# Half of the output matrix loaded during the RWKV recurrence, the other half first in the output stage

## What is computed

```python
mla_o = _mla_attend(q_nope, q_rope, kv[..., :MLA_NOPE], k_rope, kv[..., MLA_NOPE:])
hg_o, hg_s = _hgrn_mixer(hg_cols, p['hg_lb'], p['hg_norm'], hg_s0)
rw_o, rw_s = _rwkv_mixer(rw_cols, p['rw_mu'], p['rw_w0'], ..., rw_s0)
mix = jnp.concatenate([mla_o, hg_o, rw_o], axis=-1) @ p['w_out']
x = _layernorm(DEEPNORM_ALPHA * x + g1 * mix, p['ln_g'][0], p['ln_b'][0])
h2 = x * (1 + sc2) + sh2
ffn = _expert_choice(h2, p['router'], p['ex_w1'], p['ex_w3'], p['ex_w2'])
x = _layernorm(DEEPNORM_ALPHA * x + g2 * ffn, p['ln_g'][1], p['ln_b'][1])
```

## Time and profile before

| | before |
|---|---|
| timed runs, median (range) | 3454.83 us (3450.43 to 3464.23) |
| profiled execution, its own time | 3457.51 us |
| span of the profiled execution | 3455.7 us |
| mean granted TensorE clock | 0.91 |
| busy: TensorE, VectorE, GpSimd, ScalarE | 2651.1, 1272.5, 682.6, 475.0 us |
| output matmuls (line 1979) in both layers: busy, idle before them | 142.9 us, 25.1 us |
| what ended that idle time | the load of `w_out` |

### The profile page before, as it was taken

One profiled execution on the slowest core, in us unless ns is written; L12 is line 12 of the kernel. 1 busy time (PEld: TensorE's weight loads), 2 busy tenths in 40 slices (PEclk: granted clock), 3 DMA queues, 4 the chain that ended last, 5 costly groups with the idle time before them and its releaser, 6 DMA issues. The chain is left out here.

```text
span 3455.7 us, 87591 instructions
## 1 busy us (share of the span) xinstructions
PE 2651.1 (77%) x40000; PEld 2021.6 (58%) x40000; DVE 1272.5 (37%) x2847; ACT 475.0 (14%) x973; POOL 682.6 (20%) x844
## 2 busy tenths in 40 slices
PE   5998883748584888888979988566585858888886
PEld 1555553638534777777725545355484457777774
DVE  1101568784523112211240026786744231112114
ACT  0102332032101000000010023302211100000001
POOL 0000908334221000000010027272430200000001
PEclk9999997869886999999999999877798879999998
DMA  8300000000053988888671010000003458888872
GB/s 350 125 25 36 1 1 11 1 7 4 3 219 139 363 339 338 308 333 325 248 301 61 4 36 1 9 3 7 2 3 123 182 188 321 344 343 335 337 287 105
DMA packets 69616, 532.75 MB, mean 154 GB/s; under 512 B 13920, under 2 KB 15776, under 8 KB 32896
## 3 DMA queue, kind: packets, MB, share of 16 engines
q1 hardware_dynamic: 66176, 516.66, 38.4%
q0 software_dynamic: 3072, 10.49, 1.1%
HBM read 518.34 MB, written 8.79 MB: 153 GB/s over the span
## 5 line engine op out<-in xcount | busy, mean ns | idle before, releaser
L2285 PE MATMUL ps<-arena 128*64 128x80 f32 x16384 | 620.0, 235 | 107.3 <-issue 102.6
L2285 PEld LDWEIGHTS ps<-arena 128*64 128x64 f32 x16384 | 596.0, 139 | 130.0 <-issue 128.4
L2300 PE MATMUL ps<-arena 128*64 128x80 f32 x8192 | 324.2, 234 | 55.5 <-issue 53.8
L2300 PEld LDWEIGHTS ps<-arena 128*64 128x64 f32 x8192 | 304.0, 138 | 66.0 <-issue 65.7
L526 PE MATMUL ps<-arena 128*128 128x128 f32 (+1 forms) x1088 | 296.4, 435 | 5.3 <-DVE arena L579 5.3
L2470 DVE TENSOR_TENSOR arena<-arena,ps 128x160 f32<-128x160 f32 x128 | 41.2, 322 | 653.4 <-ACT arena L2390 653.4
L526 PEld LDWEIGHTS ps<-arena 128*128 128x128 f32 x1088 | 164.8, 192 | 137.0 <-issue 131.2
L2044 POOL DMA_INDIRECT arena<-h_d,arena x32 | 39.8, 1243 | 1025.9 <-DVEq L2411 920.9
L2390 ACT ACTIVATE arena<-ps 128x160 f32<-128x160 f32 x128 | 38.8, 303 | 1132.8 <-PE ps L2285 1132.8
L583 DVE COPY arena<-ps 128x128 f32<-128x128 f32 (+3 forms) x48 | 16.3, 341 | 399.4 <-PE ps L526 287.6
L1979 PE MATMUL ps<-arena 128*128 128x512 f32 x320 | 142.9, 610 | 25.1 <-DMA arena<-in_w_out 25.1
(11 more groups left out here) (345 smaller groups left out, 4065.3 us busy)
## 6 DMA issues: line engine op xcount, KB each, us to landing
arena<-in_ex_w SPq DMA_DIRECT2D x128, 2048.0 KB, 9.1
arena<-in_ex_w SPq DMA_DIRECT2D x128, 1024.0 KB, 9.2
arena<-in_ada_w SPq DMA_DIRECT2D x24, 2048.0 KB, 15.5
arena<-in_w_t SPq DMA_DIRECT2D x34, 512.0 KB, 3.5
arena<-in_w_out SPq DMA_DIRECT2D x4, 2048.0 KB, 10.3
arena<-in_w_tok SPq DMA_DIRECT2D x2, 3712.0 KB, 16.9
h_d<-x_sb SPq DMA_DIRECT2D x10, 512.0 KB, 2.6
arena<-in_w_uq SPq DMA_DIRECT2D x2, 1536.0 KB, 6.5
```

What stands on the lines that cost most here:

```text
L2285: m = nc.tensor.matmul(gated(j)[c * 64:(c + 1) * 64, f, a, :], w13[q % WG][:, a, k, f * P + c * 64:f * P + (c + 1) * 64], xT[:, x % 2, k, ...
L2300: m = nc.tensor.matmul(product(j)[c * 64:(c + 1) * 64, b, :], w2[:, q % WP, f, b * P + c * 64:b * P + (c + 1) * 64], he[:, x % 2, f, :], s ...
```

## The change

`w_out` is laid out in memory with each column half contiguous (16 KB in each partition). The first half is loaded in the RWKV stage, once SyncE has seen the last update of the inverse (`xy` = 25): its slices 0 to 5 go to the words of `rwT` from `a1` + 4 x 643, and slices 6 and 7 to the 1024 words of `hgT` from `a0` + 2560. The semaphore `ld_wo0` lives over both layers and is never cleared, so TensorE waits for 32 more in each layer. In the output stage the second half is the first request of SyncE, then the gate and norm rows, and only then come the clears, ahead of the expert weights. The small tiles of the stage lie elsewhere in the arena; their instructions are the same.

```diff
-        "w_out": f("w_out"), "ln_g": f("ln_g"), "ln_b": f("ln_b"),
+        "w_out": f("w_out").reshape(DEPTH, KD, P, 2, 512).transpose(0, 2, 3, 1, 4), "ln_g": f("ln_g"), "ln_b": f("ln_b"),
@@ phase_rwkv, SyncE
             sp.dma_start(S0, d["s_rw"][l].rearrange("d a p v -> p (d a) v")).then_inc(S["ld_rw"], 16)
+            sp.wait_ge(S["xy"], LVC * TILES)
+            k = 0
+            for dst in first_half(e):
+                n = dst.shape[1]
+                sp.dma_start(dst, d["w_out"][l, :, 0, k:k + n, :]).then_inc(S["ld_wo0"], 16)
+                k += n
             sp.wait_ge(S["rw_fin"], 1)
@@
+def first_half(e):
+
+    return e.part(e.a1 + 4 * PAD, 6, 512)[0], e.part(e.a0 + 4 * P * TILES, 2, 512)[0]
@@ phase_output
-    z = e.a0
-    wo, z = e.part(z, 2, KD, 512)
-    brow, z = e.part(z, 2, DM)
-    gb, z = e.part(z, 2, DM)
-    y, z = e.part(z, 2, DM)
+    wo_a, wo_b = first_half(e)
+    brow, z = e.part(e.a0, 2, DM)
     st, z = e.part(z, TILES, 16)
+    assert z <= e.a0 + 4 * P * TILES
+    gb, z = e.part(e.a0 + 4 * P * TILES + 2 * 512, 2, DM)
+    assert z <= e.a1 + 4 * PAD
+    y, z = e.part(e.a1 + NRW * PAD, 2, DM)
+    wo_1, z = e.part(z, KD, 512)
@@ SyncE
-            e.clear_last(sp)
-            for n in range(2):
-                sp.dma_start(wo[:, n], d["w_out"][l].rearrange("(k p) n -> p k n", p=P)[:, :, n * 512:(n + 1) * 512]
-                             ).then_inc(S[f"ld_wo{n}"], 16)
+            sp.dma_start(wo_1, d["w_out"][l, :, 1]).then_inc(S["ld_wo1"], 16)
             load_gate_rows(e, sp, 0, brow, S["n1ld"])
             load_norm_rows(e, sp, 0, gb, S["n1ld"])
+            e.clear_last(sp)
@@ TensorE
-                    if t == 0:
-                        pe.wait_ge(S[f"ld_wo{n}"], 16)
+                    if t == 0 and n == 0:
+                        pe.wait_ge(S["ld_wo0"], 32 * (l + 1))
+                    if t == 0 and n == 1:
+                        pe.wait_ge(S["ld_wo1"], 16)
```

More of the change, by code:

```diff
@@ L266, in program @@
         S = {n: sem(n) for n in ("ld_cond", "st_y")}
-        S.update({n: ctx.enter_context(nc.semaphore(n)) for n in ("ld_const", "ld_x0", "ld_x1") + EXPERT_WEIGHT_SEMS + MODULATION_WEIGHT_SEMS})
+        S.update({n: ctx.enter_context(nc.semaphore(n)) for n in ("ld_const", "ld_x0", "ld_x1", "ld_wo0") + EXPERT_WEIGHT_SEMS + MODULATION_WEIGHT_SEMS})
         e = Shared()
@@ L1931 @@
 OUTPUT_SEMS = (
-    "n1x", "op_ps", "op_ev", "st_x", "n1ld", "n1var", "n1sd", "n1nm", "n1xn", "ld_wo0", "ld_wo1",
+    "n1x", "op_ps", "op_ev", "st_x", "n1ld", "n1var", "n1sd", "n1nm", "n1xn", "ld_wo1",
 )
@@ L1975, in _ @@
                 for n in range(2):
-                    if t == 0:
-                        pe.wait_ge(S[f"ld_wo{n}"], 16)
+                    if t == 0 and n == 0:
+                        pe.wait_ge(S["ld_wo0"], 32 * (l + 1))
+                    if t == 0 and n == 1:
+                        pe.wait_ge(S["ld_wo1"], 16)
                     for k in range(KD):
-                        m = nc.tensor.matmul(ps[:, 2 * (t % 4) + n, :], e.mixT[:, k, t * P:(t + 1) * P], wo[:, n, k, :],
+                        half = wo_1[:, k, :] if n else wo_a[:, k, :] if k < 6 else wo_b[:, k - 6, :]
+                        m = nc.tensor.matmul(ps[:, 2 * (t % 4) + n, :], e.mixT[:, k, t * P:(t + 1) * P], half,
                                              start=k == 0, stop=k == KD - 1)
```

## The result

| | before | after |
|---|---|---|
| timed runs, median (range), 7 each | 3454.83 us (3450.43 to 3464.23) | 3428.47 us (3422.20 to 3440.66) |
| ratio, 95% interval | | 0.9923 (0.9909 to 0.9938) |
| span of the profiled execution | 3455.7 us | 3429.4 us |
| output matmuls in both layers: busy, idle before them | 142.9, 25.1 us | 142.8, 2.1 us |

The change saves 0.77%, 26 us; the forecast was 3432.2 us, 0.65% less. In two later comparisons the same kernel came out at 0.9939 (0.9925 to 0.9952) and 0.9935 (0.9916 to 0.9953) of the kernel before. The mean of the three ratios, 0.9932, is 23.4 us of 3454.8, and the forecast was 22.6.

A forecast was written before the change was run, and what follows sets the result against it. TensorE's stall before each layer's first output matmul, ended by the matrix load, was taken as on the path. 3457.5 - 11.5 - 11.1 = 3434.9, less 2.7 for the median, gave 3432.2 us; range 3425 to 3443.

The forecast's parts named there:

- The seam: Between RWKV and output stages, TensorE starts at the barrier instead of the load: gains 11.54 and 11.07 us, 22.6 together.
- The path argument: Output stage is TensorE-bound, so an earlier start moves tiles, barrier and rest of layer equally; the stall counts fully, twice.
- The term of the barrier: Gap from RWKV's last instruction to TensorE's first output matmul, taken as 0.5 us from the preceding seam's 0.28 and 0.69.
- The second half: Requested first in the output stage, lands after 8.2 us, before the first matmul group's 10.2 and 9.3 us end.
- Rival 1: Second half takes 12.8 us to land, stalling TensorE 3.0 and 3.9 us inside tile 0; 3439.1 us; chance 0.13.
- The estimate of 6.8 us: Second half's landing time by the skill's 2.0 us plus bytes / 436 GB/s; the sum would stay unchanged.
- The other requests: Output stage's gate and norm rows, last out near 954.0, and expert weights, near 958.6, behind the clears; cost 0.
- The recurrence: In the RWKV stage, the early load slows nothing: 0, with a far bound of 2 us a layer.
- The clock: At the output stage's start, low clock keeps costing 3.36 and 2.44 us; twice as long a stretch costs 5.8 us.
- a bound of 3.2 us: No low-clock stretch in tile 0 would gain 5.8 us, less the second half late by 1.3 us twice.
- Rivals 2 and 3: 2: TensorE tied elsewhere or experts' stage returns gain, near 3451, chance 0.07; 3: clock stays low, 3563, chance 0.03.

The follow-up runs named there:

- The run with the clears ahead: Changed kernel with the 64 semaphore clears put back ahead of the output stage's requests; 3436.82 us, ratio 0.9947.
- eight times the data: Changed kernel with each of the two pieces of the first half loaded eight times in the recurrence, 16 MB instead of 2 MB; 3429.84 us, ratio 0.9927.
- the 15 dummies: Changed kernel plus 15 unused matmuls on TensorE between the RWKV stage's transposes of the final state and of the result; 3429.32 us, ratio 0.9934.
- The run with 96 transposes: Changed kernel with both halves loaded early and 96 dummy transposes of a constant in place of the 15 dummy matmuls; single run 3426.39 us.
- with both halves early: Changed kernel with 15 dummy matmuls and the second half requested at the recurrence's end; 3423.66 us, ratio 0.9917; again 3426.97 us, 0.9920.
- seven dummies: Changed kernel with both halves loaded early and 7 dummy matmuls instead of 15; single run 3425.32 us.
- the order alone changed: Kernel before with the 64 clears moved after the matrix and row requests, nothing loaded early; 3453.76 us, ratio 0.9990.

## Why the prediction was right

**The seam.** 22.6 us forecast, 22.98 measured. The path argument held: all of it reached the end of the stage, whose rest kept its length (86.01 and 85.46 us). The term of the barrier was sized at 0.5 us between 0.28 and 0.69, and was 0.32 and 0.31; this 0.4 us is the only error in the sum proper.

**The second half.** Forecast to be in time by 2.0 and 1.1 us, with 7.8 us to landing and 0.4 for the issue. It landed 7.2 and 7.4 us after its request, and no wait is seen. The run with the clears ahead measured what happens without the margin: 2.13 and 1.07 us of wait. Rival 1 is refuted: its 12.8 us belonged to a load that had 2 MB ahead of it. The estimate of 6.8 us used a fit that the Trainium skill, "DMA: Bandwidth & Descriptors", section "Anatomy of one DMA — SWDGE (gpsimd) path", gives for loads issued by GpSimd. These are issued by SyncE, and the measured 7.2 to 7.4 us decide; by either figure the load is hidden.

**The other requests.** They cost nothing, as forecast, but were sized too long. The last norm row went out at 949.01 and not near 954.0, and landed 12.0 us later, at 961.0, 3 us before tile 0 was done. The expert weights were asked for from 953.42 on, against 958.6 forecast.

**The recurrence.** Forecast at 0 with 2 us a layer as the far bound; eight times the data showed 0.01 and 0.06 us between two profiles with the same clock. The forecast did not name what goes with a longer recurrence, a low clock at its start: 83.76 us beside 79.38 in two profiles of the changed kernel.

**The clock.** Forecast unchanged. Tile 0 changed by -0.30 and +0.08 us. The size was right: the 15 dummies show that the level at the seam is set by TensorE's rest of 12.7 us before the transposes, which the change leaves as it was, and not by the pause of the seam. That the low stretch could be removed, which I had only as a bound of 3.2 us, turned out to be worth 6.6 to 6.9 us, because the transposes of the result speed up too (1.1 us a layer) and the second half can be moved as well. The dummies alone gave 5.3. My sentence that the 0.50 in the transposes agrees with the Trainium skill, "TensorE: Matmul & The Clock Gate", part "PE-mode transpose", was a weak reading: they stood low because TensorE had rested ahead of them, and ten of them are over in 2.4 us. The run with 96 transposes speaks against the rule for 32-bit transposes in this kernel, as far as keeping the clock at 1.00 goes; that transposes alone raise it from 0.50 no run here shows.

**Rivals 2 and 3.** The seam is ended by the barrier, the experts' stage is not longer (table below), and the clock rose after 5.5 us: both are out.

**What the sum does not hold.** The profiled spans differ by 26.3 us, the seams by 22.98 and tile 0 by 0.2. The other 3.1 us lie in the other stages. The distances between SyncE's first requests of stages (for RWKV, from its first load to the store of the final state) show the scatter, in us, over the 14 profiles of this study (three without an early half, eleven with it; two layers each):

| stage | without, 6 values | with, 22 values |
|---|---|---|
| RWKV | mean 236.9, 233.9 to 241.7 | mean 237.4, 234.3 to 241.2 |
| experts | mean 602.5, 597.0 to 605.9 | mean 599.0, 593.7 to 604.9 |
| attention | mean 206.8, 206.6 to 207.0 | mean 205.1, 202.3 to 207.1 |

The RWKV stage is the same. The experts' and the attention stage look shorter with the change by 3.5 and 1.7 us. Twice that would be 10 us beyond the seams, while the mean timed ratio leaves 0.4 us beyond them. For the attention stage the record speaks against a real effect: the one of layer 0 runs before the first instruction that the change touches, and there the difference is largest (206.9 without, 204.6 with). Its length goes with the granted clock, 0.97 in the profiles of 202.3 to 203.6 us and 0.95 or 0.96 in those of 206.7 us and more. The RWKV stage scatters in the same way, from 0.86 at 233.9 us to 0.83 at 241.7. In the experts' stage the clock (0.97 to 0.99) goes with the length far less, and whether there is a small real effect is left open; six values are few, and no run here was made to isolate it.

**The range.** 3425 to 3443 held 3428.47 and the later 3433.54 and 3429.28.

## What to carry to other kernels

A load that is asked for at the start of a stage and wanted by its first instruction costs its whole landing time there (7.8 us here), and a list of housekeeping instructions ahead of the request is added to it. Ask for the part that the first matmuls use one stage earlier, into memory that the trace and the code show to be out of use, and size that part so that its work covers the landing of the rest: here 9 to 10 us of matmuls over 7.2 to 7.4 us of landing. Then read what the engine meets next, which here was the low clock, and give the engine something to do in the wait right before the seam. Each microsecond that the first part gets faster comes off the cover of the load behind, so ask for that one earlier too: here the dummies alone gave 5.3 us and with both halves early 6.9.

## What the runs showed of the hardware

- 188 GB/s into the arena for 90 us, at a DMA share of 0.56, left a chain of TensorE, VectorE, ScalarE and GpSimd instructions the same to 0.1 us a step, beside a profile with the same granted clock (0.92).
- The same kernel's recurrence takes 78.1 to 83.8 us from profile to profile. In the longest ones the granted clock is 0.52 for 6 to 10 us at its start, and the same happens with no load in flight (0.51, 82.0 us).
- TensorE's granted clock stayed at 1.00 for over 4 us of rest (seven dummies: end 938.06, still 1.00 at 942) and was 0.50 by 944. In the kernel before it fell sooner: end 932.34, fall between 935 and 936. Back-to-back transposes of 128 x 128 held it at 1.00 for 10.6 us.
- A stage seam with a barrier of all engines costs 0.30 to 0.32 us from the last instruction to TensorE's first, in all twenty-two seams of the profiles with the first half early.
- The four gate and norm row requests took SyncE 1.9 us (947.54 to 949.45) after one request of 16 KB a partition, and 5.5 us (953.39 to 958.85) after two requests in 2 KB pieces; in layer 1 of the kernel before it was 4.7 us. I had sized them at 5.5 us. With the order alone changed they took 5.6 us again (949.68 to 955.33), so it is not the clears; the size of the pieces or the amount queued remain, and the runs don't part them.
- Clearing 64 semaphores took SyncE 3.97 us in layer 0 (949.45 to 953.42) and 3.56 in layer 1, 62 and 56 ns each. Why the layers differ is not shown.
